# Recurrence chunks: direction 1's products in the off-diagonal quadrants, issued alternately with direction 0's

## What is computed

```python
def step(S, inp):
    w_t, k_t, v_t, kk_t, a_t = inp[:5]
    sa = jnp.einsum('bhvk,bhk->bhv', S, kk_t)
    S = (S * w_t[:, :, None, :] - sa[..., None] * (kk_t * a_t)[:, :, None, :]
         + v_t[..., None] * k_t[:, :, None, :])
    return S, (jnp.einsum('bhvk,bhk->bhv', S, inp[5]) if emit else None)
...
s_fwd, yc_fwd = wkv7_scan(zero, cx, 0, False, need_ctx)
s_bwd, yc_bwd = wkv7_scan(zero, cx, 1, True, need_ctx)
_, y_fwd = wkv7_scan(s_fwd, lat, 0, False, True)
_, y_bwd = wkv7_scan(s_bwd, lat, 1, True, True)
```

## Time and profile before

| | |
|---|---|
| median of 3 runs | 4833.1 us (4823.01 to 4834.37) |
| profiled execution | 4830.95 us, span 4829.2 us |
| busy: PE, PEld | 4169.2 us (86%), 3611.0 us (75%) |
| busy: DVE, ACT, POOL | 2249.1 us (47%), 1458.7 us (30%), 595.7 us (12%) |
| mean granted PE clock | 0.918 |
| the stage of `rwkv_chunks` | 1728 to 2165 us, 437 us |

### The profile page before, as it was taken

One profiled execution on the slowest core, in us unless ns is written; L12 is line 12 of the kernel. 1 busy time (PEld: TensorE's weight loads), 2 busy tenths in 40 slices (PEclk: granted clock), 3 DMA queues, 4 the chain that ended last, 5 costly groups with the idle time before them and its releaser, 6 DMA issues. The chain is left out here.

```text
span 4829.2 us, 85278 instructions
## 1 busy us (share of the span) xinstructions
PE 4169.2 (86%) x35880; PEld 3611.0 (75%) x35880; DVE 2249.1 (47%) x3566; ACT 1458.7 (30%) x2464; POOL 595.7 (12%) x749
## 2 busy tenths in 40 slices
PE   6786799999977668888998875799999995859999
PEld 5554588888964468886998765788888893548998
DVE  4454443334635644445444434443336854854444
ACT  2254321213234412113222333421123333633222
POOL 2010100001101332211000101100001102520000
PEclk8888899999988789998999887899999997869999
DMA  4446322222347831204332326322222344533332
GB/s 163 139 145 201 128 61 65 60 64 66 121 153 235 277 108 45 50 26 133 95 94 73 104 86 173 128 61 62 66 60 68 108 132 141 178 126 101 96 92 83
DMA packets 677460, 527.29 MB, mean 109 GB/s; under 512 B 124157, under 2 KB 600609, under 8 KB 677120
## 3 DMA queue, kind: packets, MB, share of 16 engines
q1 hardware_dynamic: 652800, 450.46, 31.1%
q0 software_dynamic: 24320, 71.89, 4.1%
HBM read 440.23 MB, written 82.01 MB: 108 GB/s over the span
## 5 line engine op out<-in xcount | busy, mean ns | idle before, releaser
L87 PE MATMUL acc<-h_hi,w_hi 128*128 128x258 f32 (+2 forms) x4416 | 1394.9, 316 | 45.0 <-DVE w_lo L478 33.0
L89 PE MATMUL acc<-h_hi,w_lo 128*128 128x258 f32 (+2 forms) x4416 | 1391.4, 315 | 0.0
L88 PE MATMUL acc<-h_lo,w_hi 128*128 128x258 f32 (+2 forms) x4416 | 1390.0, 315 | 0.0
L87 PEld LDWEIGHTS acc<-h_hi,w_hi 128*128 128x128 f32 x4416 | 833.2, 189 | 108.2 <-DVE w_lo L478 34.3
L88 PEld LDWEIGHTS acc<-h_lo,w_hi 128*128 128x128 f32 x4416 | 833.9, 189 | 57.8 <-issue 0.5
L89 PEld LDWEIGHTS acc<-h_hi,w_lo 128*128 128x128 f32 x4416 | 833.5, 189 | 56.1
L478 DVE TENSOR_TENSOR w_lo<-staged,w_hi 128x1024 fp32r<-128x1024 f32 (+1 forms) x414 | 488.4, 1219 | 137.1 <-ACT w_hi L356 134.0
L356 ACT CAST w_hi<-staged 128x1024 fp32r<-128x1024 f32 (+1 forms) x414 | 407.3, 1028 | 460.0 <-PE acc L89 363.6
L519 DVE COPY offset<-acc 128x2 f32<-128x2 f32 x276 | 43.7, 158 | 919.9 <-PE acc L89 916.8
L87 PE MATMUL acc<-hidden_hi,w_hi 128*128 128x512 f32 (+1 forms) x1200 | 420.2, 350 | 44.4 <-DVE hidden_lo L613 44.2
L88 PE MATMUL acc<-hidden_lo,w_hi 128*128 128x512 f32 (+1 forms) x1200 | 419.6, 350 | 0.0
(11 more groups left out here) (473 smaller groups left out, 6143.6 us busy)
## 6 DMA issues: line engine op xcount, KB each, us to landing
staged<-in_w_ffn_in SPq DMA_DIRECT2D x88, 512.0 KB, 4.5
staged<-in_ffn_w_in SPq DMA_DIRECT2D x88, 512.0 KB, 4.7
wmod<-in_w_mod SPq DMA_DIRECT2D x8, 3072.0 KB, 11.2
wmod<-in_mod_w SPq DMA_DIRECT2D x8, 3072.0 KB, 13.1
wmod<-in_mod_w SPq DMA_DIRECT2D x16, 1536.0 KB, 10.4
staged<-in_ssd_w_in SPq DMA_DIRECT2D x42, 512.0 KB, 4.5
rows<-acum SPq DMA_DIRECT2D x40, 512.0 KB, 5.3
wmod<-in_w_mod SPq DMA_DIRECT2D x8, 2048.0 KB, 8.1
```

Of the source, the lines that this page charges most:

```text
L87: nc.tensor.matmul(out, w[0], x[0], start=start, stop=False)
L88: nc.tensor.matmul(out, w[0], x[1], start=False, stop=False)
L89: return nc.tensor.matmul(out, w[1], x[0], start=False, stop=stop)
```

## The change

Direction 1's products take the other two quadrants: `product` and `turn` put the output of corner `c` on corner `1 - c` where `turned` is set. The new helper `both` issues, for each `h`, two products of direction 0 and two of direction 1. It takes the place of two calls of `each` for all products but `z_p`, the last ones with `state`, and the turned `ar` and `vf` in part. A product of a tile whose halves are exchanged gives one whose halves are not, so these lie right again. For direction 1 there is one more product, `be` by `ar` without exchange into `big` (in `betas_with`), from which VectorE makes `z`; its turned `ar` goes into `big` too.

PE now waits once for both directions ahead of such a call: for the later of the two. The wait for `z_c` is followed by a wait for `alpha_c` of the next step, since `big` is used twice, and the products with `state` wait for PE's own `sums_p` and `reads_p`. VectorE does both additions to `x`, then both to `z`, then both directions' masks.

```diff
-                        for c in corners:
-                            mm = nc.tensor.matmul(out[c, h], lhs[c, h], rhs[c, h], start=start and (stop or h == 0),
-                                                  stop=stop and (start or h == H - 1))
+                def product(out, lhs, rhs, h, c, turned, start, stop):
+
+                    return nc.tensor.matmul(out[corners[1 - c if turned else c], h], lhs[corners[c], h], rhs[corners[c], h],
+                                            start=start and (stop or h == 0), stop=stop and (start or h == H - 1))
...
+                def both(out, lhs, rhs, name, start=True, stop=True):
+
+                    apart()
+                    for h in range(H):
+                        for d in range(2):
+                            for c in range(2):
+                                mm = product(out[d], lhs[d], rhs[d], h, c, d == 1, start, stop)
+                            if name and h == H - 1:
+                                mm.then_inc(S[name], 1)
...
+                def betas_with(i, s, latent):
+                    wait(pe, "mp_ready", i, 1)
...
+                    each(big[1][:, :, 0, :], be[s][1], ar[s][1][:, :, 0, :], "bar")
+
+                def turn_betas(i, s, latent):
+                    wait(pe, "lt_ready", i, 1)
                     if latent:
+                        pe.wait_ge(S["q_ready"], 2 * i + (2 - 2 * CC))
+                    turn_both(side(front, 0), be[s], None)
+                    turn_both(side(front, 1), ka[s], "bk_t")
...
+                    for h in range(H):
+                        for c in range(2):
+                            turn(front[0][:, :, 0, :], ar[s][0][:, :, 0, :], h, c, False)
+                        for c in range(2):
+                            turn(front[1][:, :, 1, :], vf[s][1], h, c, True)
+                    for h in range(H):
+                        for c in range(2):
+                            tr = turn(front[0][:, :, 1, :], vf[s][0], h, c, False)
+                    tr.then_inc(S["av_t"], 1)
+                    for h in range(H):
+                        for c in range(2):
+                            tr = turn(big[1][:, :, 1, :], ar[s][1][:, :, 0, :], h, c, False)
+                    tr.then_inc(S["av_t"], 1)
...
+                        else:
+                            wait(pe, "x_c", i, 1, n - 1, LEV - 1)
+                            wait(pe, "z_c", i, 1, n - 1, LEV)
+                        both(one, [lev[s][d][n] for d in range(2)], x[s], "lx_p")
+                        if ahead and n < 4:
+                            (keys_with, betas_with, turn_betas, turn_values)[n](i + 1, s1, next_latent)
+                        if n == 0:
+                            wait(pe, "mv_c", i, 1)
+                        wait(pe, "lx_c", i, 1, n, LEV)
+                        if n < LEV - 1:
+                            both(six, z[s], lx, "x_p")
+                        for d in range(2):
+                            each(one[d], lx[d], z[s][d], "z_p")
+                    wait(pe, "z_c", i, 1, LEV - 1, LEV)
+                    if ahead:
+                        wait(pe, "alpha_c", i + 1, 1)
+                    both(pairs(big), z[s], pairs(am[s]), "au_p")
...
                     for n in range(LEV):
-                        for d in range(2):
-                            if n < LEV - 1:
+                        if n < LEV - 1:
+                            for d in range(2):
                                 wait(dve, "x_p", i, d, n, LEV - 1)
...
+                        for d in range(2):
                             wait(dve, "z_p", i, d, n, LEV)
...
-                            if ahead and n < 2:
+                        if ahead and n < 2:
+                            for d in range(2):
                                 (mask_keys, mask_betas)[n](i + 1, s1, d, next_latent)
```

More of the change, by code:

```diff
@@ L2078, in core @@
-                    for d in range(2):
-                        wait(pe, "z_c", i, d, LEV - 1, LEV)
-                        each(pair(big[d]), z[s][d], pair(am[s][d]), "au_p")
-                    for d in range(2):
-                        each(one[d], kt[s][d], vt[s][d], None, stop=False)
-                        if latent:
-                            each(six[d], vt[s][d], mp[s][d][:, :, 1, :], None, stop=False)
-                    if ahead:
-                        for d in range(2):
-                            turn_inverse(i + 1, s1, d)
@@ L2088, in core @@
-                    for d in range(2):
-                        wait(pe, "au_c", i, d)
-                        if latent:
-                            each(pair(big[d]), au[d][:, :, 0, :], pair(bq[s][d]), "gf_p")
-                        else:
-                            each(big[d][:, :, 0, :], au[d][:, :, 0, :], bq[s][d][:, :, 0, :], "gf_p")
-                    for d in range(2):
-                        each(one[d], bq[s][d][:, :, 0, :], au[d][:, :, 1, :], None, start=False, stop=False)
-                        if latent:
-                            each(six[d], au[d][:, :, 1, :], bq[s][d][:, :, 1, :], None, start=False, stop=False)
@@ L2098, in core @@
-                    for d in range(2):
-                        wait(pe, "gf_c", i, d)
-                        if fresh(i):
-                            pe.wait_ge(S["cleared"], 2)
-                        each(one[d], grow[d], state[d], None if latent else "core_p", start=False)
-                        if latent:
+                    wait(pe, "mp_ready", i, 1)
+                    wait(pe, "v_c", i, 1)
+                    if latent and not (type(i) is int and i <= CC):
+                        pe.wait_ge(S["y_c"], 2 * i - 2 * CC)
@@ new lines, in core @@
+                    wait(pe, "z_c", i, 1, LEV - 1, LEV)
+                    if ahead:
+                        wait(pe, "alpha_c", i + 1, 1)
+                    both(pairs(big), z[s], pairs(am[s]), "au_p")
+                    both(one, kt[s], vt[s], None, stop=False)
+                    if latent:
+                        both(six, vt[s], side(mp[s], 1), None, stop=False)
+                    if ahead:
+                        turn_inverse(i + 1, s1)
+                    wait(pe, "au_c", i, 1)
@@ new lines, in core @@
+                    if latent:
+                        both(pairs(big), side(au, 0), pairs(bq[s]), "gf_p")
+                    else:
+                        both(side(big, 0), side(au, 0), side(bq[s], 0), "gf_p")
+                    both(one, side(bq[s], 0), side(au, 1), "sums_p", start=False, stop=False)
+                    if latent:
+                        both(six, side(au, 1), side(bq[s], 1), "reads_p", start=False, stop=False)
+                    wait(pe, "gf_c", i, 1)
+                    if fresh(i):
+                        pe.wait_ge(S["cleared"], 2)
@@ L2104, in core @@
+                    wait(pe, "sums_p", i, 1)
+                    if latent:
+                        pe.wait_ge(S["reads_p"], 2 * i + (2 - 2 * CC))
+                    for d in range(2):
+                        each(one[d], grow[d], state[d], None if latent else "core_p", start=False)
+                    if latent:
+                        for d in range(2):
                             each(six[d], state[d], read[d], "core_p", start=False)
                 for part in (keys_with, betas_with, turn_betas, turn_values):
-                    for d in range(2):
-                        part(0, 0, d, False)
@@ L2109, in _ @@
-                for d in range(2):
-                    turn_inverse(0, 0, d)
+                    part(0, 0, False)
+                turn_inverse(0, 0)
                 chunks(pe, core)
```

103 lines of the change are left out of this document (47 added, 56 removed).

## The result

The changed kernel takes 4862.8 us (median of 5 runs, 4857.24 to 4867.84), the kernel before in the same session 4832.0; the ratio is 1.0068 with a 95% interval of 1.005 to 1.0086. It is slower by 0.7%: inside the forecast's range (4800 to 4885), but not where the forecast put it. It said 4830 and gave "slower" 0.31; the time went up by 31 us.

A forecast was written before the change was run, and what follows sets the result against it. It took delivery of instruction blocks to bound 64-column pairs, the array only 128-column ones. Latent steps -6, context steps +2 and the last step +1 summed to -3 us: 4830 us, range 4800 to 4885.

The forecast's parts named there:

- slower: Two rival cases, quadrants not working four at a time (0.20) and a lower clock (0.11): together chance 0.31.
- Packing: Products of both directions in four array quadrants: a 64-column pair of calls takes 0.6 us instead of 0.93.
- Waits merged: PE waits for both directions before their products: middle level 4.1 us, level 2 6.9, level 4 3.4.
- chain of a latent step: Dependent work and waits through mv, the levels and the closing part of a latent step: 32.7 us by itself.
- second rival: Quadrants take turns, pairs stay at 0.93 and 1.75 us, merged waits are paid: about +50, 4883 us, chance 0.20.
- Against the delivery: Latent step: instruction blocks need 34.8 us, the chain 32.7; blocks decide, plus 1.9 gives 36.7, say 36.6.
- At least 4.42 us a block: PE's program arrives in blocks of about 124 products' records, each costing at least 4.42 us, 1.14 a pair.
- cross-sum on the kernel before: Check on a latent step before the change: 960 records make 7.74 blocks, 34.2 us of a measured 37.4.
- third rival: Half-idle PE falls to 1.2 GHz in one or two stretches a step: +11 to +22 us, chance 0.11.
- Context steps: Four context steps: blocks 31.4 us against a chain of 28.5, plus 1.9 gives 33.3; +0.6 each, +2 in all.
- What would show it: Signs if right: blocks of 4.3 to 4.6 us, issue waits above 100 us, PE busy down a quarter, 91 to 92 blocks.

The follow-up runs named there:

- e15: Changed kernel plus nine or ten wide, never-read products a step (128x128 by 256 columns), sized to end inside PE's waits: 4844.9 us.
- e1: Changed kernel with every product writing to its own half of the partitions again (quadrants on the diagonal), all else kept: 4870.9 us.
- e16: Changed kernel plus as many never-read products at the same places as e15, but 64x64 by 16 columns: 4851.5 us.
- e4: Kernel before with each complete product and each turn cut to half its columns: 4903.5 us.
- e7: Kernel before plus 62 tiny products (64x64 by 16 columns) in each of eleven steps, ahead of level 2's turns: 4888.9 us.
- e11: e9 plus two wide, never-read products a level in PE's wait for ScalarE's copies of lx: 4841.8 us.
- e9: Changed kernel with the next step's products issued behind each level's z products, VectorE's lt and bq masks of both directions first, z masks a level later: 4815.9 us.

## Why the prediction was wrong

**Packing: right, and better than taken.** 0.47 us a pair, not 0.6. It leaves the array idle the more.

**Waits merged: right, with sizes a little long.** Level 2 at full clock is 6.1 to 6.3 us in e15's latent steps, for 6.9; two levels of the changed kernel's last step are 3.84 and 3.92 for a middle level's 4.1, its level 4 3.26 for 3.4. The chain of a latent step is at most the 32.7 us of the forecast. What merged waits and order cost without the packing was worked out for the second rival at +50 and came as +48 in the steps (e1).

**Against the delivery: this step failed.** It set 32.7 of chain beside 34.8 of blocks and let the larger decide, because "the chain's long wait (level 2) lets one block come ahead". In the profile they come nearer to adding. A block in which PE waited 2.3 us and which lasted 7.74 was followed by a stall of 1.12 like its neighbours of 3.79 and 3.93, and five more like it were too. In the seven latent steps the stalls for late instructions are 44.3 us (the 51.6 of issue less 7.3 that were waits for z), 6.3 a step: chain 32.7 + 6.3 makes 39.0, where the forecast had 34.8 of blocks + 1.9 = 36.7; measured are 41.4 (289.8 / 7). The 2.4 that remain, or more where the chain is long, are of the size of the low clock's price: 12 us of it a step, at the estimated 0.13 to 0.26, are 1.6 to 3.2.

The premise of that step failed too. "At least 4.42 us a block" was the mean of three windows taken for a lower bound: a block came after 3.98 in the trace of the kernel before and after 3.79 in the changed one. And a 64-column pair was not bound by delivery in the latent steps of the kernel before, where eight blocks in a row, 4.76 us each, passed without a stall. A shorter block would have made the forecast faster, so these are errors of opposite sign. The cross-sum on the kernel before (7.74 x 4.42 = 34.2 of 37.4) came out well for another reason: there 960 records at 29 ns are 28 us and the stalls and 128-column pairs fill the rest.

**The clock: seen, priced about rightly, and left out of the sum.** The third rival had one or two stretches a step for 11 to 22 us. They came, 120 us in all; the runs price 51 of them at 6.5 to 13 us, which makes 15 to 31 for all by estimate. It was entered with a chance of 0.11 as an alternative, though nothing excluded it beside the forecast's own waits: PE was to be busy a quarter less and stand 3 us in level 2 in the forecast too. The clock shows most in level 2 (1.9 us between e16 and e15). The Trainium skill ("TensorE: Matmul & The Clock Gate", "HAM oscillation — how this bites in real kernels") describes a matmul engine that falls back to the low clock in waits for a DMA; here the same happens in waits for VectorE, and in e4 with 21 us of waits in 494, by narrow products.

**Context steps** were forecast at +2 us in all and came at +7.5, for the same reason: 28.5 + 4.7 of late instructions (18.9 / 4) is 33.2, measured 34.6.

What closes the account of +31 us: taking away the z masks from PE's way gives 22 back, and the forecast had that wait in its chain; it was not the size of the wait that was missed but that nothing made up for it. How the loss divides between late blocks and low clock stays open. Nearly every edit that moved one moved the other; in the nearest to a clean pair (e15, e16) 51 us less of low clock go with 6.5 us of time. That each block's fetch begins only late in the block before is what the windows suggest; no run tested it.

The signs in "What would show it" were half met: records at 15 ns and PE busy down by 18% (not a quarter), 91 blocks as said; but blocks under 4 us, issue waits 79 (65 without those for z) and not above 100, and a clock of 0.85 in the latent steps.

## What to carry to other kernels

When a change makes an engine's work shorter, ask for each wait whether it is covered, and add the uncovered ones: a stall for instructions came here behind a wait for another engine and not under it, so the step was nearer to the sum than to the larger. Before making PE faster, move its filling work to the longest wait: the packing with its merged waits cost 31 us, the same with the filling work behind z and the masks reordered gained 13. Price the parts of such a change one by one: here the packing itself gained some 8 us and the waits and order that came with it cost 40. And when an idle time is called issue, look whether an operation that the engine needs ended just before its start. A side effect that the forecast's own numbers imply (half-idle PE, so a lower clock) belongs in the sum, not among the alternatives.

## What the runs showed of the hardware

- Products of 64x64 weights take the same time with 64, 32 or 16 columns: 29 ns a record with two quadrants in turn (e4, e7). With four quadrants in turn a record of 64 columns comes every 15 ns.
- A busy PE did not keep the clock: with half the columns and PE busy 95% of the time it was 0.65 on average (e4), with full columns and PE busy 89% it was 0.99 (the kernel before).
- The closest that blocks of instructions followed each other between stalls was 3.79 us in the changed kernel and 3.47 in e16, and one came 1.12 us late although the block before it had lasted 7.74.

```profile
1762.25:1765.72 3.47, 2.60 (x127) 2.52 (x127) 0.75 (x2) 1.85 (x6) 1.80 (x3) 1.00 0.06 15
```

- A wide filler of 128x128 by 256 columns costs about 0.48 us, and with what stands around it two of them fill 1.2 us; e11, where they overran their wait by 0.2 us a level, was 26 us slower than e9.
